# 64-dimensional heads on two halves of the array; x tile 1 turned first; MLA low parts and copies in another order

## The reference

```python
# DSA: 16 heads of 64, 4 key heads; indexer of 8 heads of 64
s = jnp.einsum('bqhd,bsd->bqhs', iq_b, ik) * IDX_DIM ** -0.5
score = jnp.einsum('bqh,bqhs->bqs', iw_b, jax.nn.relu(s))
_, sel = lax.top_k(score, top_k)                      # causal, 64 keys per query
logits = jnp.einsum('bqgrd,bqkgd->bqgrk', q_b, k_sel) * A_HEAD_DIM ** -0.5
o = jnp.einsum('bqgrk,bqkgd->bqgrd', jax.nn.softmax(logits), v_sel)
...
# MLA: 8 heads, 128 dimensions without rotation and 64 with, one rotated key for all
s = (jnp.einsum('bqhd,bkhd->bhqk', qn, k_nope)
     + jnp.einsum('bqhr,bkr->bhqk', qr, k_rope)) * scale
o = jnp.einsum('bhqk,bkhd->bqhd', jax.nn.softmax(causal(s)), v)
```

## Time and profile before

| | |
|---|---|
| three runs | 1289.73, 1290.10, 1293.04 us |
| their median | 1290.1 us |
| time of the profiled execution | 1293.0 us |
| its span, first to last instruction | 1291.3 us |
| mean granted TensorE clock | 0.996 |
| busy: PE, PEld | 98%, 86% |
| busy: DVE, ACT, POOL | 67%, 46%, 7% |

### The profile page before, as it was taken

The page is one execution under the profiler, slowest core; times in us unless marked ns, Lnnn a source line. Parts: engine busy times, 40 slices in busy tenths (PEclk is TensorE's granted clock), DMA queues, the critical chain, the costliest instruction groups (busy, mean ns, idle before and its releaser), DMA issues.

```text
span 1291.3 us, 17135 instructions
## 1 busy us (share of the span) xinstructions
PE 1269.5 (98%) x7225; PEld 1108.2 (86%) x7225; DVE 868.0 (67%) x928; ACT 589.5 (46%) x715; POOL 90.3 (7%) x216
## 2 busy tenths in 40 slices
PE   8999999999999999999999999999999999999998
PEld 7888888888888888888888888887899988888887
DVE  5776776666666676666776666667577666666675
ACT  5663534444724444443654444435552245444334
POOL 4340000001000200000101000001000010000000
PEclk9998999999999999999999999999999999999999
DMA  8421765555633765554625655555653336665542
GB/s 270 138 92 49 246 196 195 188 185 160 204 98 130 228 196 189 187 188 145 230 66 170 197 195 195 184 181 189 211 161 102 98 131 236 196 195 185 185 152 98
DMA packets 131260, 220.93 MB, mean 171 GB/s; under 512 B 6984, under 2 KB 99424, under 8 KB 131184
## 3 DMA queue, kind: packets, MB, share of 16 engines
q1 hardware_dynamic: 128160, 209.83, 49.1%
q0 software_dynamic: 3024, 10.01, 2.6%
HBM read 218.77 MB, written 1.05 MB: 170 GB/s over the span
## 4 chain that ended last, share of the span: by engine, by line
PE 79%; DVE 8%; ACT 5%; DMA 3%; issue 2%; POOL 1%; ACTq 0%; DVEq 0%; POOLq 0%
PE ps L732 18%; PE ps L588 17%; PE ps L734 9%; PE ps L565 7%; PE ps L566 7%; PE ps L567 7%; DVE wlo L1713 4%; PE ps L693 3%; ACT whi L1269 3%; PE ps L895 3%; PE ps L746 2%; ACT rot L1294 1%; PE ps L858 1%; DMA raw<-in_mlp_w_up 1%; DMA raw<-in_ffn_w_in 1%
## 5 line engine op out<-in xcount | busy, mean ns | idle before, releaser
L1713 DVE TENSOR_TENSOR wlo<-raw,whi 128x2048 fp32r<-128x2048 f32 (+3 forms) x203 | 452.0, 2240 | 173.5 <-ACT whi L1269 171.8
L1269 ACT ACTIVATE whi<-raw 128x2048 fp32r<-128x2048 f32 (+3 forms) x203 | 377.1, 1869 | 77.3 <-DMA raw<-in_hgrn_w_in 25.3
L732 PE MATMUL ps<-xhl,whi 128*128 128x512 f32 x1088 | 271.4, 391 | 0.0
L732 PEld LDWEIGHTS ps<-xhl,whi 128*128 128x128 f32 x1088 | 198.3, 188 | 37.3
L588 PE MATMUL ps<-whi,xhl 128*128 128x512 f32 (+1 forms) x864 | 213.1, 380 | 5.2 <-DVE wlo L1713 2.4
L588 PEld LDWEIGHTS ps<-whi,xhl 128*128 128x128 f32 x864 | 152.7, 189 | 35.4 <-DVE wlo L1713 3.1
L565 PE MATMUL ps<-whi,hh 128*128 128x512 f32 x432 | 169.0, 391 | 0.0
L566 PE MATMUL ps<-whi,hl 128*128 128x512 f32 x432 | 168.6, 390 | 0.0
L567 PE MATMUL ps<-wlo,hh 128*128 128x512 f32 x432 | 168.1, 389 | 0.0
L734 PEld LDWEIGHTS ps<-xhl,wlo 128*128 128x128 f32 x1088 | 148.4, 190 | 10.6
L734 PE MATMUL ps<-xhl,wlo 128*128 128x256 f32 x1088 | 151.7, 282 | 0.0
(11 more groups left out here) (323 smaller groups left out, 1376.9 us busy)
## 6 DMA issues: line engine op xcount, KB each, us to landing
raw<-in_ffn_w_in SPq DMA_DIRECT2D x44, 1024.0 KB, 5.1
raw<-in_mlp_w_up SPq DMA_DIRECT2D x32, 1024.0 KB, 5.3
raw<-in_mlp_w_down SPq DMA_DIRECT2D x32, 1024.0 KB, 4.8
raw<-in_ffn_w_down SPq DMA_DIRECT2D x22, 1024.0 KB, 4.9
raw<-in_hgrn_w_in SPq DMA_DIRECT2D x16, 1024.0 KB, 5.5
raw<-in_b_w_in SPq DMA_DIRECT2D x12, 1024.0 KB, 5.3
raw<-in_ple_w_gate SPq DMA_DIRECT2D x8, 1024.0 KB, 6.7
raw<-in_a_w_in SPq DMA_DIRECT2D x6, 1024.0 KB, 5.4
```

The lines of the kernel that those rows point to most:

```text
L732: mm(bank(b + f), w[0][:, kk, P * f : P * f + P], xhl[:, kk, :, :].rearrange("p a n -> p (a n)"), start=(kk == 0), stop=False)
L1269: a.activation(whi[:, slot, 0:w], raw[:, slot, 0:w], ACT.Copy).then_inc(s["hi_done"], 1)
L1713: v.tensor_tensor(wlo[:, slot, 0:w], raw[:, slot, 0:w], whi[:, slot, 0:w].bitcast(F32), ALU.subtract).then_inc(s["lo_done"], 1)
```

## The change

- **Halves.** The indexer's scores (all units) and the logits of DSA and the rotated part of MLA (units with b = 1) read 64 rows: `head_rows(h)` is rows 0 to 63 for an even head and 64 to 127 for an odd one. Heads of the two halves follow each other and write different PSUM banks; `PLACE` gives the place of a head in the logits. `INDEX_UNITS` gives even and odd heads to different units, and two units are issued in turn. The indexer's keys `ikT` lose their zeros: one copy of 128 partitions on ACT instead of two of 64, and no memset of 128x512 on POOL.
- **MLA logits of b = 1** go by pairs: two products over 128 rows, then two over 64 rows.
- **Start.** PE turns x tile 1 before it multiplies tile 0, four `keep_fed` transposes fall away, and DVE makes the low part of chunk 1 before the angles.
- **MLA.** DVE makes the low part of `mla_kv` chunk 0 before it rotates the second half of the queries. ACT makes the high parts of the first two chunks of `mla_o` after the copies that the first logits need, not before.
- **PLE.** DVE makes the low part of the next input's tile 0 before the third quarter's product, not after it.

The core of the diff (the new places are used in the same way in MLA's `turn_probs` and `exps`):

```diff
@@ -260,7 +260,7 @@
         kT = buf[4][:, :].rearrange("p (g e n) -> p g e n", g=A_KV, e=2)
-        ikT = half(7, 0)[:, 0:512].rearrange("p (e n) -> p e n", e=2)
+        ikT = half(7, 0)[:, 0:SEQ]
@@ -334,6 +334,12 @@
         QUERY_ROWS, QUERY_COLUMNS = (0, 4), (2, 6)
+        PLACE = ((0, 1, 2, 3), (0, 2, 1, 3))
+        def logit_out(b, i):
+            return ps[:, 0, P * i : P * i + P] if b == 0 else ps[:, 2 + i % 2, 256 * (i // 2) : 256 * (i // 2) + 256]
@@ -444,7 +450,6 @@
-            note(g.memset(ikT[:, :, :], 0.0))
@@ -559,6 +564,10 @@
             mm = nc.tensor.matmul
+            def head_rows(h):
+                return slice(64 * (h % 2), 64 * (h % 2) + 64)
@@ -826,8 +835,7 @@
                         n = P * (b + 1)
-                        o = ps[:, 0, P * h : P * h + P] if b == 0 else ps[:, 2 + h // 2, 256 * (h % 2) : 256 * (h % 2) + 256]
-                        last = score_mm(o, b, 4 * g + h, n)
+                        last = score_mm(logit_out(b, h), b, 4 * g + h, n)
@@ -838,7 +846,7 @@
                         for h in range(4):
-                            src = logit4[u % 4][:, P * nk * h + P * kt : P * nk * h + P * kt + P]
+                            src = logit4[u % 4][:, P * nk * PLACE[b][h] + P * kt : P * nk * PLACE[b][h] + P * kt + P]
@@ -927,11 +935,11 @@
             keep_fed(12)
+            turn_tile(T_X0, x, 0)
+            keep_fed(16)
+            turn_tile(T_X0, x, 1)
+            take(first["dsa_iq"])
             for tt in range(TT):
-                turn_tile(T_X0, x, tt)
-                keep_fed(16 - 12 * tt)
-                if tt == 0:
-                    take(first["dsa_iq"])
@@ -973,14 +981,18 @@
-            for u, (b, hs) in enumerate(INDEX_UNITS):
+            for u in range(0, len(INDEX_UNITS), 2):
+                b, hs = INDEX_UNITS[u]
                 if u >= 4:
-                    pe.wait_ge(s["index_relu"], u - 3)
+                    pe.wait_ge(s["index_relu"], u - 2)
                 n = P * (b + 1)
-                for i, h in enumerate(hs):
-                    last = mm(ps[:, 4 + u % 4, n * i : n * i + n], iqT[:, h // 2, b * P : b * P + P], ikT[:, h % 2, 0:n], start=True, stop=True)
-                last.then_inc(s["index_scores"], 1)
+                for i in range(len(hs)):
+                    for e in range(2):
+                        h = INDEX_UNITS[u + e][1][i]
+                        last = mm(ps[:, 4 + (u + e) % 4, n * i : n * i + n], iqT[head_rows(h), h // 2, b * P : b * P + P], ikT[head_rows(h), 0:n], start=True, stop=True)
+                        if i == len(hs) - 1:
+                            last.then_inc(s["index_scores"], 1)
@@ -1007,7 +1019,8 @@
             def dsa_scores(o, b, h, n):
-                return mm(o, qT[:, h // 2, b * P : b * P + P], kT[:, h // 4, h % 2, 0:n], start=True, stop=True)
+                r = head_rows(h) if b == 1 else slice(0, P)
+                return mm(o, qT[r, h // 2, b * P : b * P + P], kT[r, h // 4, h % 2, 0:n], start=True, stop=True)
@@ -1115,11 +1128,15 @@
                 n = P * (b + 1)
-                for i in range(4):
-                    h = 4 * g + i
-                    o = ps[:, 0, P * i : P * i + P] if b == 0 else ps[:, 2 + i // 2, 256 * (i % 2) : 256 * (i % 2) + 256]
-                    mm(o, qnT[:, h, b * P : b * P + P], knT[:, h, 0:n], start=True, stop=False)
-                    last = mm(o, qrT[:, h // 2, b * P : b * P + P], krT[:, h % 2, 0:n], start=False, stop=True)
+                group = 1 + b
+                for i0 in range(0, 4, group):
+                    for i in range(i0, i0 + group):
+                        h = 4 * g + i
+                        mm(logit_out(b, i), qnT[:, h, b * P : b * P + P], knT[:, h, 0:n], start=True, stop=False)
+                    for i in range(i0, i0 + group):
+                        h = 4 * g + i
+                        r = head_rows(h) if b == 1 else slice(0, P)
+                        last = mm(logit_out(b, i), qrT[r, h // 2, b * P : b * P + P], krT[r, h % 2, 0:n], start=False, stop=True)
@@ -1379,8 +1396,8 @@
                     for h in range(4):
-                        v = logit4[u % 4][:, n * h : n * h + n]
-                        last = a.activation(v, v, ACT.Exp, bias=negmax[:, u % 4, h : h + 1], accum_out=rowsum[:, b, 4 * g + h : 4 * g + h + 1])
+                        v = logit4[u % 4][:, n * PLACE[b][h] : n * PLACE[b][h] + n]
+                        last = a.activation(v, v, ACT.Exp, bias=negmax[:, u % 4, PLACE[b][h] : PLACE[b][h] + 1], accum_out=rowsum[:, b, 4 * g + h : 4 * g + h + 1])
@@ -1491,10 +1508,7 @@
                 a.activation(iqT[:, :, P * tt : P * tt + P], bank(6 + tt).rearrange("p (k n) -> p k n", k=4), ACT.Copy).then_inc(s["indexT_done"], 1)
-                for e in range(2):
-                    r = slice(64 * e, 64 * e + 64)
-                    last = a.activation(ikT[r, e, P * tt : P * tt + P], ps[r, 4 + tt, 0:P], ACT.Copy)
-                last.then_inc(s["indexT_done"], 1)
+                a.activation(ikT[:, P * tt : P * tt + P], ps[:, 4 + tt, 0:P], ACT.Copy).then_inc(s["indexT_done"], 1)
@@ -1627,7 +1641,6 @@
                 two_banks(qnT, c, QUERY_COLUMNS[c], "qn_out")
-            ahead(first["mla_q"] + 2)
@@ -1636,8 +1649,9 @@
             query_parts(0)
-            ahead(first["mla_kv"] + 1)
+            ahead(first["mla_q"] + 1)
             query_parts(1)
+            ahead(first["mla_q"] + 2)
@@ -1993,7 +2007,6 @@
                         ahead(n0 + 3)
-                    if layer == 0 and u == 3:
@@ -2002,6 +2015,7 @@
             turned(T_X0, 1)
+            until(first["dsa_iq"] + 1)
@@ -2015,7 +2029,7 @@
                 v.tensor_scalar(cs[:, :, :], cs[:, :, :], PI_MAX, -PI_MAX, ALU.min, ALU.max).then_inc(s["angle_done"], 1)
-                until(first["dsa_iq"] + 1 + w)
+                until(first["dsa_iq"] + 2 + w)
@@ -2195,6 +2209,7 @@
                     1, cosM, sinM).then_inc(s["kr_rotated"], 1)
+            ahead(first["mla_down"] + 2)
@@ -2283,7 +2298,7 @@
-INDEX_UNITS = [(0, [0, 1, 2, 3]), (0, [4, 5, 6, 7])] + [(1, [2 * i, 2 * i + 1]) for i in range(4)]
+INDEX_UNITS = [(0, [0, 2, 4, 6]), (0, [1, 3, 5, 7]), (1, [0, 2]), (1, [1, 3]), (1, [4, 6]), (1, [5, 7])]
```

More of the change, by code:

```diff
@@ L1130, in turn_probs @@
                     for i in range(4):
-                        src = logit[:, u % 2, P * (b + 1) * i + P * kt : P * (b + 1) * i + P * kt + P]
+                        src = logit[:, u % 2, P * (b + 1) * PLACE[b][i] + P * kt : P * (b + 1) * PLACE[b][i] + P * kt + P]
                         last = nc.tensor.transpose(ps[:, (1, 4, 1, 2)[u] + kt, P * i : P * i + P], src, ident[:, :])
@@ L1602, in exps @@
                 for i in range(4):
-                    v = logit[:, u % 2, n * i : n * i + n]
-                    last = a.activation(v, v, ACT.Exp, bias=negmax[:, u % 2, i : i + 1], accum_out=rowsum[:, b, 4 * g + i : 4 * g + i + 1])
+                    v = logit[:, u % 2, n * PLACE[b][i] : n * PLACE[b][i] + n]
+                    last = a.activation(v, v, ACT.Exp, bias=negmax[:, u % 2, PLACE[b][i] : PLACE[b][i] + 1], accum_out=rowsum[:, b, 4 * g + i : 4 * g + i + 1])
                 last.then_inc(s["m_exp"], 1)
```

## The result

The changed kernel takes 1280.1 us (median of 4 runs, 1279.1 to 1282.0), the kernel before 1290.8 (4 runs). The ratio is 0.9916, with a 95% interval of 0.9898 to 0.9935: some 10.7 us less, where the sum of the forecast was 7.6.

What follows compares the result with a forecast made beforehand. The prediction took PE as the bound, busy nearly all of 1291.3 us. Terms of 0.9, 1.6, 1.9, 2.35 and 0.85 sum to 7.6 us, from 1291.5 to 1283.9 (likeliest 1284), range 1280 to 1289.

Steps and rivals of the forecast that it cites:

- three upper bounds: Low end of the range: start 1.3 us more, changes free 0.3, an execution with the full clock 1.5.
- The sum: Whole kernel: start 0.9, indexer 1.6, attention 1.9, MLA order 2.35 and PLE 0.85 give 7.6 us less.
- Start: Kernel start: PE has chunks 1 and 2 earlier, at 13.3 and 17.6; 0.9 us less, bounds 0.5 and 2.2.
- Indexer: Indexer scores: 8 heads of b = 1 save 0.21 us each, less two changes; 1.6 us less.
- Attention: DSA attention: logits of unit 1 bring 0.43 us, units 5 and 7 0.84 each, less changes; 1.9 us less.
- Changes of mode: PE, between 128 and 64 rows: one change costs 0 to 0.16 us, taken as 0.05.
- MLA halves: MLA logits of b = 1: done before DVE comes to them, so nothing either way.
- MLA order: MLA: PE's waits of 1.70 and 0.65 us go; 2.35 us less, bounds 1.0 and 2.6.
- PLE: Behind the PLE: PE's wait of 0.87 us for tile 0's low part goes; 0.85 us less.
- The halves don't overlap: Indexer and attention: 3.5 us less gain and up to 1.6 for changes, 1287.4 to 1289; chance 0.19.
- The clock falls longer: Attention: faster logits lengthen PE's waits, a second slow stretch costs up to 5.1 us, 1289; chance 0.17.
- the slower case: Attention: clock stays at 1.2 GHz from near 77 us to 107, 14 us more, 1298; chance 0.06.

Runs made afterwards that it cites:

- the one-half kernel: The changed kernel with every head's queries and keys taken from rows 0 to 63 where it takes halves; 1285.4 us, ratio 0.9971.
- the order alone: The kernel before with only the order of MLA's low parts and copies changed; 1286.3 us, ratio 0.9975.
- the late copy: The changed kernel with DVE's copy of unit 5's probabilities done twice; four executions 1280.6 to 1281.2 us, eight 1285.6 to 1288.6.
- DVE's part alone: The kernel before with only MLA's low part put ahead of the rotation of the queries on DVE; 1290.1 us, ratio 0.9998.

## Why the prediction was off

- **The start of the sum failed: "Since the new kernel will also have executions of both kinds, I take it from the mean of the four times, 1291.5".** I saw two slow times of four and took them for half. The profiled execution (1293.0) may well be the 1293.04 of the three runs, counted twice. Falls are 18 of 85; without them the kernel before takes 1288.9, 2.6 less than I started from. And none of the changed kernel's nine counted executions falls. I also took a mean where the result is a median, which one fall in five hardly moves (1289.3 with the falls on one chip, 1289.15 without). I had read what PE did ahead of the fall (idle 0.8 of 4 us, matmuls of 64 columns), but treated it as something that the change leaves alone or makes worse. The wait there fell from 1.06 to 0.92, and with it the fall went. That is 2.6 of the 3.9 us by which I was off. The cost of a change of mode, which I had only as a loss, is what shortened the wait. That the measured 1280.1 still stands at the very end of my range of 1280 to 1289 is luck: the full clock was there as 1.5 us, one of three upper bounds that would all have had to come together.
- **The sum** was 7.6, measured 8.3 to 8.8 without a fall: 8.3 on one chip, 8.4 by the parts, 8.8 over all chips.
- **Start**: 0.9 forecast, 1.28 between the profiled executions and 1.1 by traces of one chip, 0.4 by the medians. PE had chunk 1 at 12.84 (13.3 forecast), chunk 2 at 17.14 (17.6). Another trace of the same kernel has 13.75 and 18.05, so the times themselves agree to no better than a microsecond. The delay came from where I put it, ACT behind the angles.
- **Indexer**: 1.6 forecast, 1.66 measured, for a partly wrong reason. I wrote that "loads still come one after the other" and that the units of 128 keys gain nothing. The windows of PE over the two parts, before and after:

```profile
45.00:46.80 1.80, 1.80 (x18) 1.00 0.33 50
46.80:50.10 3.30, 3.30 (x18) 1.00 0.75 293
```

```profile
43.78:44.78 1.00, 1.00 (x17) 1.00 0.00 0
44.78:47.18 2.40, 2.10 (x20) 1.00 0.88 259
```

  The 16 matmuls of 128 columns took 1.8 us and take 1.0: loads of two halves run side by side as well. That is the step that failed here; the rows that I had showed no loads of two halves, and their loads all had 128 rows. A load of 64 rows costs the same 0.11 us by itself, as the one-half kernel shows. The units of 256 keys brought 0.9, not 1.7, since PE now waits 0.30 for ACT at 46.12 and restarts. A gain and a wait that I had missed cancelled.
- **Attention**: 1.9 forecast, 1.93 measured.
- **Changes of mode**: 0.05 each taken, more measured. In the changed kernel a DSA unit of 256 keys starts at 85.56 and what follows at 86.63: 1.07 us for four pairs, where four steps of 0.215 (eight of them took 1.78 between starts before) make 0.86. So 0.2 for the two changes, 0.1 each. The Trainium skill (TensorEngine Tiling (Array Packing), Key Properties) says that a change of mode drains the engine; the trace agrees, with that price.
- **MLA halves**: nothing forecast, nothing measured (the order alone brings the same 2.85). The logits of b = 1 take 3.28 us between starts with halves and 4.14 on one half, where 16 steps of 0.215 without any change of mode make 3.44. So the halves there pay for little more than their own changes of mode.
- **MLA order**: 2.35 forecast, 2.85 measured. Both waits went, and each was worth 0.15 more than its printed length (1.86 and 0.80 us beyond the usual step, between the starts on either side), since the first matmul behind a wait shows a longer step. That makes 2.66; the other 0.2 is not traced. DVE needed the low parts later than ACT delivered them, as forecast.
- **PLE**: 0.85 forecast, 1.0 in the trace, 0.7 by the medians.
- **Rivals**: "The halves don't overlap" is refuted by the one-half kernel. "The clock falls longer" came out the other way round: fewer falls. But the mechanism is real, and the late copy and DVE's part alone show its price. Nothing spoke for the slower case.

## What to carry to other kernels

If the executions of one kernel differ in their mean clock, count both kinds over many executions before the base of a sum is chosen, and look in the trace for the wait behind which the clock falls: shortening it can be worth more than its length; filling it took the falls away here but cost 0.4 to 1 us. Here two heads of 64 on two halves of the array save close to half of their matmuls' time, at 128 columns too, less 0.1 us for each change of mode, so they belong in blocks and not between matmuls of 128 rows. When one wait on PE is removed, look at what PE asks for next and remove that in the same edit, or the time only moves.

## What the runs showed of the hardware

- TensorE's clock fell from 2.4 to 1.2 GHz behind waits of only 1.06 to 2.37 us, and only in some executions. One fall in the attention cost 4.2 us between the same points.
- Matmuls on different halves ran side by side even when four on one half were queued between them. The Trainium skill (TensorE: Matmul & The Clock Gate, The mechanism) says that matmuls start and end strictly in program order; the counts of 4 and then 11 starts per 0.55 us do not fit that. Single starts could be misplaced in the profile, but the 3.54 us for all 32 against 5.50 on one half could not.
- Chunk 1 reached PE between 15.56 and 16.50 us in seven traces whose start was that of before. The lag arises in the first transposes: they come 0.21 us apart, and from 4.6 us on 0.11 in the kernel before, but from 6.0 to 7.5 us on in the six others, although the granted clock reads 1.00 there. A lead or lag of a microsecond from the start is carried to the end, and is the size of the effects looked for there.
